# Input weights of two layers multiplied as high and low rounded parts, in a smaller ring of weight slots

## What is computed

```python
for layer in range(2):
    h = rms_norm(x, norm1_g[layer])
    sb, rw, mc, hc = h @ w_l[:, 0:768], h @ w_l[:, 768:1792], h @ w_l[:, 1792:2560], h @ w_l[:, 2560:3584]
    merged = None
    for n, y_n in enumerate((y_sb, y_rwkv, y_moba, y_hgrn)):       # the four mixers' outputs
        gate = jax.nn.sigmoid(h @ w_l[:, 3584 + 1024 * n:4608 + 1024 * n])
        term = gate * (y_n @ w_branch[layer, n])
        merged = term if merged is None else merged + term
    x = x + merged @ w_out[layer]
    h2 = rms_norm(x, norm2_g[layer])
    x = x + (silu(h2 @ w_ffn_gate[layer]) * (h2 @ w_ffn_up[layer])) @ w_ffn_down[layer]
```

## Time and profile before

| | us |
|---|---|
| median of 3 runs | 2181.14 (2177.85 to 2185.31) |
| profiled execution, its own time | 2176.91 |
| span in its profile | 2175.1 |

### The profile page before, as it was taken

How to read it: one execution, slowest core, us unless ns; L and a number is a source line. 1 busy time by engine, 2 the same in 40 slices (tenths; PEclk the granted TensorE clock), 3 DMA queues, 4 the chain that set the end, 5 groups by cost and what they waited for, 6 DMA issues and landing times.

```text
span 2175.1 us, 26152 instructions
## 1 busy us (share of the span) xinstructions
PE 1915.3 (88%) x11290; PEld 1442.1 (66%) x11290; DVE 771.7 (35%) x1306; ACT 524.1 (24%) x784; POOL 0.2 (0%) x4
## 2 busy tenths in 40 slices
PE   7999999999998999998999999998999876565654
PEld 6799876799997898766799998546888421111111
DVE  3442332655533533234355665323544200000001
ACT  2201121244432011211344463423442210000000
POOL 0000000000000000000000000000000000000000
PEclk9999999999999999999999999999999897677778
DMA  6222342465532223453745442211127799999997
GB/s 249 97 97 87 127 155 97 155 193 186 183 117 97 97 97 116 155 194 136 240 155 174 158 129 64 97 39 39 40 78 306 304 409 409 409 409 409 409 409 291
DMA packets 170323, 414.13 MB, mean 190 GB/s; under 512 B 4832, under 2 KB 61408, under 8 KB 166752
## 3 DMA queue, kind: packets, MB, share of 16 engines
q1 hardware_dynamic: 169488, 408.69, 50.8%
q10 hardware_dynamic: 720, 3.78, 0.4%
HBM read 411.41 MB, written 1.05 MB: 190 GB/s over the span
## 4 chain that ended last, share of the span: by engine, by line
PE 60%; DMA 20%; DVE 12%; ACT 7%; issue 1%; SPq 0%; ACTq 0%; DVEq 0%
PE ps L219 44%; PE ps L767 7%; DMA ring<-in_w_e_down_dram 5%; ACT rarena L213 5%; DMA high<-in_w_e_up_dram 5%; DVE rarena L178 4%; PE ps L1157 3%; PE ps L1514 2%; DVE low L178 2%; DMA ring<-in_w_e_up_dram 2%; DMA high<-in_w_e_down_dram 2%; DMA high<-in_w_e_gate_dram 2%; DMA ring<-in_w_e_gate_dram 2%; DVE high L178 2%; ACT high L213 1%
## 5 line engine op out<-in xcount | busy, mean ns | idle before, releaser
L219 PE MATMUL ps<-high,ring 128*128 128x256 f32 (+1 forms) x2016 | 482.7, 391 | 7.5 <-DMA ring<-in_w_in_dram 5.6
L219 PE MATMUL ps<-rarena 128*128 128x256 f32 (+1 forms) x3648 | 460.0, 288 | 9.6 <-DVE rarena L178 7.4
L219 PEld LDWEIGHTS ps<-rarena 128*128 128x128 f32 x3648 | 448.3, 192 | 19.6 <-DVE rarena L178 10.4
L219 PEld LDWEIGHTS ps<-high,ring 128*128 128x128 f32 x2016 | 376.4, 192 | 81.4 <-issue 20.2
L213 ACT ACTIVATE high<-ps 128x512 f32<-128x512 f32 (+2 forms) x210 | 103.3, 492 | 719.0 <-PE ps L1514 286.8
L1514 PE MATMUL ps<-high,low 128*32 128x512 f32 x1040 | 168.2, 780 | 103.0 <-DMA high<-in_w_e_up_dram 36.4
L178 DVE TENSOR_TENSOR rarena<-ring,rarena 128x2048 fp32r<-128x2048 f32 x76 | 167.3, 2201 | 137.5 <-ACT rarena L213 135.8
L1514 PEld LDWEIGHTS ps<-high,low 128*32 128x32 f32 x1040 | 32.1, 129 | 224.0 <-issue 62.0
L213 ACT ACTIVATE rarena<-ring 128x2048 fp32r<-128x2048 f32 x76 | 140.0, 1841 | 157.0 <-DMA ring<-in_w_ffn_up_dram 92.7
L178 DVE TENSOR_TENSOR high<-high,ps 128x512 f32<-128x512 f32 x52 | 35.7, 687 | 324.8 <-PE ps L1514 267.0
L219 PE MATMUL ps<-low,ring 128*128 128x256 f32 (+1 forms) x544 | 128.0, 392 | 14.9 <-DVE low L192 5.5
(11 more groups left out here) (149 smaller groups left out, 1364.9 us busy)
## 6 DMA issues: line engine op xcount, KB each, us to landing
ring<-in_w_in_dram SPq DMA_DIRECT2D x34, 2048.0 KB, 7.9
high<-in_w_e_gate_dram SPq DMA_DIRECT2D x22, 2048.0 KB, 24.0
high<-in_w_e_up_dram SPq DMA_DIRECT2D x22, 2048.0 KB, 24.1
high<-in_w_e_down_dram SPq DMA_DIRECT2D x21, 2048.0 KB, 24.0
ring<-in_w_mod_dram SPq DMA_DIRECT2D x12, 2048.0 KB, 8.7
ring<-in_w_ffn_gate_dram SPq DMA_DIRECT2D x22, 1024.0 KB, 5.4
ring<-in_w_ffn_up_dram SPq DMA_DIRECT2D x22, 1024.0 KB, 8.0
ring<-in_w_e_down_dram SPq DMA_DIRECT2D x11, 2048.0 KB, 24.3
```

Source lines behind the costliest of these rows:

```text
L219: ins = self.e.matmul(out, l, r, start=first and i == 0, stop=end and i == n - 1)
```

## The change

The 52 units of each layer are multiplied in parts, as the feed-forward part is. One piece is a block of 128 columns (128x1024 elements). ScalarE rounds it into slot 2 of the ring, which becomes the store of high parts (four places for blocks 0 to 27, two places after that, since half of the slot is needed), and VectorE writes the low part over the weights in their own slot. ScalarE does this for block u+2 in the first half step of unit u, VectorE in the second; from block 30 on it is block u+1. The input `h` is split as well, tile by tile during `rp`. In the mixers' stretch weights thus come through two slots, 0 and 1. The other half of slot 2 holds the branch weights `b1`, and then the modulation, in 24 loads of 1 MB one after the other, with a step of 4 matmuls each, spread over five gates after every 4 half steps (layer 0) or every 2 (layer 1). The branch weights `b0` go to slot 2 after the last mixer step. One `yield` of the RWKV mixer on ScalarE moves ahead of its `kn` work, and `MX_PLAN` is lengthened.

```diff
-            def units(l, nm, c0, w, parts):
-                wt = halves(wslot(f"{l}w{c0}")[:, 0:8 * w], 8)
-                PE.wait_ge(f"{l}w{c0}")
+            def units(l, nm, parts):
+                b_ = first_block[nm]
...
-                        prs = [(wt[:, j, o:o + 128], B.h[:, j, :]) for j in range(8)]
+                        ld, z, lo, hi_ = block_of(l, b_)
+                        PE.wait_ge(f"{l}lo{b_}")
+                        prs = [(hi_[:, j, :], lo[:, j, :], hh_[:, j, :], hl_[:, j, :]) for j in range(8)]
...
-                    PE.group(out, prs[0:4], end=False)
+                    PE.group3(out, prs[0:4], end=False)
...
+def blocks_ahead(u):
+
+    if u + 2 < TWO_PLACES + 2:
+        return [u + 2]
+    return [u + 1] if TWO_PLACES < u < BLOCKS - 1 else []
...
+            def block_high(l, b):
+
+                ld, z, low_, high_ = block_of(l, b)
+                A.wait_ge(ld, f"{fname(l - 1, FJOBS[-1])}.used" if l else None)
+                if b > 3:
+                    A.wait_ge(f"{l}blk{b - (4 if b < TWO_PLACES + 2 else 2)}.used")
+                A.act(fr(high_), z, Copy).then_inc(*A(f"{l}hi{b}"))
...
+            def block_low(l, b):
+
+                ld, z, low_, high_ = block_of(l, b)
+                V.wait_ge(f"{l}hi{b}")
+                low_part(low_, z, high_, f"{l}lo{b}")
...
-                for _ in mods:
-                    pass
+                ring_of[0] = NSLOT
+                held[2] = f"{l}fill.used"
                 for n in (0, 2, 3):
                     branch(l, n)
...
+                yield
                 A.wait_ge(f"{l}kn.ps")
                 A.wait_ge(f"{l}kmax")
                 A.act(R.t2, R.t2, Ln).then_inc(*A())
                 A.act(R.t1, R.t2, Exp, scale=-0.5).then_inc(*A(f"{l}kn"))
-                yield
...
+                h_low(7)
+                block_low(l, 0)
+                block_low(l, 1)
...
-MX_PLAN = 10 * [2] + [1], 14 * [2] + [1]
+BLOCKS, TWO_PLACES = 52, 28
+MX_PLAN = 13 * [2] + [1], 22 * [2] + [1]
```

More of the change, by code:

```diff
@@ L268, in mix, with woven, beside @@
             n += 1
-def woven(parts, other, counts):
-    for part, n in zip(parts, counts):
-        yield from part
-        for _ in range(n):
-            next(other, None)
-            yield
+def woven(parts, other, every):
+    n = 0
+    for part in parts:
+        for _ in part:
+            yield
+            n += 1
+            if n % every == 0:
+                next(other, None)
+                yield
[3 more added lines that the diff above has]
+    return [u + 1] if TWO_PLACES < u < BLOCKS - 1 else []
+def beside(steps, split, u, half):
+    for n, _ in enumerate(steps):
+        if n % 2 == half:
+            for b in blocks_ahead(u + n // 2):
+                split(b)
+        yield
 class Space:
@@ L391, in build @@
         B.xg = B.mg
+        place["top"] = GATES_AT
+        hh_ = shaped(rgates[:, :].bitcast(F32), [8, 256])
         B.gates = alloc(8, 256)
@@ L395, in build @@
         B.rs = alloc(256)
+        hl_ = shaped(rarena[:, place["top"] - LOW:place["top"] - LOW + 2048].bitcast(F32), [8, 256])
         B.h = alloc(8, 256)
@@ L443, in build @@
         free_to(mark)
-        gx = [B.gates] + [alloc(8, 256) for _ in range(2)]
+        gx = [at(23304, 8, 256)] + [alloc(8, 256) for _ in range(2)]
         H = Space()
@@ L679, in sync_program @@
                     table["par"] = (s_par, 32)
-                mods = modulation(l)
-                fill = [proj(l)] + [gate(l, n, ch) for n in (1, 0) for ch in range(2)]
-                fill += [woven([gate(l, n, ch) for n in (2, 3) for ch in range(2)], mods, MOD_COUNTS[l])]
-                mix([none(RW_STEPS)], fill, RW_PLAN, False)
-                branch(l, 1)
-                mix([none(HG_STEPS), none(SB_STEPS), none(MO_STEPS)], fill, MX_PLAN[l])
-                for _ in mods:
-                    pass
+                for nm, c0, w, parts in IN1:
+                    columns(f"{l}w{c0}", a["w_in"][l], c0, w)
+                for n, ch in GATES[0:3]:
+                    gate(l, n, ch)
+                held[HALF] = f"{l}blk{TWO_PLACES - 1}.used"
+                branch(l, 1, at=HALF)
+                mods = modulation(l)
+                gate(l, *GATES[3])
+                for i in range(4, 9):
+                    if i < 8:
+                        gate(l, *GATES[i])
+                    for _ in range(8 // MOD_EVERY[l]):
+                        next(mods, None)
+                ring_of[0] = NSLOT
+                held[2] = f"{l}fill.used"
                 for n in (0, 2, 3):
@@ L719, in sync_program @@
                 columns(f"to{half}", a["w_out_2"][0], 512 * half, 512)
[L721 removed]
+            ring_ = list(recent)
             order = ring_[:1] + [5, 6, 7, 8] + [3, 4] + ring_[1:]
@@ L790, in units @@
+                        PE.wait_ge(f"{l}lo{b_ + 1}")
+                        done = [b_, b_ + 1] if t else []
+                        tok = slice(128 * t, 128 * t + 128)
+                        prs = [(hh_[:, j, tok], hl_[:, j, tok], hi_[:, j], lo[:, j, :]) for j in range(8)]
+                        b_ += 2 * t
+                    PE.group3(out, prs[0:4], end=False)
                     yield
-                    PE.group(out, prs[4:8], first=False).then_inc(*PE(f"{l}{nm}{i}.ps"))
+                    PE.group3(out, prs[4:8], first=False).then_inc(*PE(f"{l}{nm}{i}.ps"))
@@ L792, in units @@
+                    for n in done:
+                        PE.mark(f"{l}blk{n}.used")
                     yield
-                PE.mark(f"{l}w{c0}.used")
+                PE.mark(f"{l}w{BLOCK[first_block[nm]][0]}.used")
             def proj(l):
                 for nm, c0, w, parts in IN1:
-                    yield from units(l, nm, c0, w, parts)
+                    yield from units(l, nm, parts)
             def gate(l, n, ch):
-                yield from units(l, f"g{n}{ch}", gate_col(n, ch), 512, "cccc")
+                yield from units(l, f"g{n}{ch}", "cccc")
@@ L1173, in tensor_program @@
                 mix([hgrn(l), stick(l), moba(l)], fill, MX_PLAN[l])
+                PE.mark(f"{l}fill.used")
                 branch(l, 0)
-                for _ in mods:
-                    pass
                 branch(l, 2, hgrn_turned)
```

134 lines of the change are left out of this document (80 added, 54 removed).

## The result

The changed kernel takes 2260.97 us (median of 4 runs, 2257.38 to 2261.64) where the kernel before takes 2180.83 beside it: the ratio is 1.036, with a 95% interval of 1.0341 to 1.0379. It is slower by 80 us. The prediction had 8 us slower and a range that ended at 2220. The direction was right, the size was not.

A forecast was written before the change was run, and what follows sets the result against it. TensorE's own work was taken as the bound, VectorE close behind after KBt. Costs of 68.7 us less 60.3 saved gave +8.4: 2185.3 us for an execution like the profiled one, 2189.5 beside the median; range 2158 to 2220.

The forecast's parts named there:

- theory A: Experiments' theory: rounding queued on VectorE and ScalarE ahead of short steps makes TensorE wait, each wait bringing a low clock.
- theory B: Experiments' theory: the loss comes from two slots and half a slot, whose loads land late.
- (a): Before kn: VectorE's low part of h and two blocks' low parts come first, delaying it 3.0 us a layer.
- (b): Before bo: ScalarE passes seven fill steps first, so TensorE waits, 6.5 us a layer with the low clock.
- (c), (d): VectorE after KBt, with six low parts, 4.2 and 1.8 us; one more low part before first X, 1.3 a layer.
- (e): Fourth level's D: late load g10, then a low part ahead of VectorE's X, cost 5.2 us a layer.
- (g): Other mixers: low parts queued ahead lengthen existing waits, and layer 0's pairs shift; 6.4 and 3.8 us.
- (h): Modulation through half a slot: waits for its chained loads, 0 us in layer 0 and 12.9 in layer 1.
- (i): Branch 0: its weights wait for slot 2, held until the last mixer step; 2.8 us a layer.
- first rival: Matmuls in parts run nearer their floor in short groups between float32 work, below 0.117 us each: 2159.5 us; chance 0.15.
- fourth: Rival: matmuls in parts get no cheaper at all, and the waits come: 2250 us; chance 0.02.
- third: Rival: the half slot's loads land late, 6.9 us for 1 MB and 10.3 for 2 MB: 2222 us; chance 0.30.

The follow-up runs named there:

- e7: Changed kernel's plan with float32 matmuls and no rounding, modulation joined to the half steps, ScalarE's kn step back ahead of the fill: 2202.0 us.
- e1: Changed kernel's slots, loads and order, but float32 matmuls straight from the slot and no rounding of weights or h: 2239.6 us.
- e2: Changed kernel with only each layer's first four blocks rounded, on ScalarE, and all 52 multiplied from those, for high and low parts alike: 2194.3 us.
- e3: Changed kernel without VectorE's low parts of the weights; ScalarE's high parts stay and are multiplied in their place: 2202.8 us.
- e14: Changed kernel without VectorE's low parts of the weights, modulation joined to the half steps, branch 0's weights in the half slot: 2172.6 us.
- e9: Changed kernel with the modulation joined to the half steps and branch 0's weights in the half slot: 2229.3 us.
- e5: Changed kernel with each modulation step joined to the half step behind it, not in a place of its own: 2246.1 us.
- e4: Changed kernel with the columns' loads an eighth and the modulation's a quarter as large, rounding and matmuls unchanged in number and shape: 2215.9 us.
- e8: Changed kernel with branch 0's weights loaded into the half slot after the last modulation step, instead of slot 2: 2244.2 us.
- e13: Changed kernel with float32 matmuls of constants put ahead of twelve of TensorE's waits: 2249.1 us.
- e10: Changed kernel with the low parts of the weights made by GpSimd instead of VectorE: 2258.3 us.

## Why the prediction was wrong

The runs make a ladder from one kernel to the other, in medians: the loads of the half slot and of branch 0, +21 (before to e7); the order, +38 (e7 to e1); the cheaper matmuls, -45 (e1 to e2); ScalarE's high parts, +8 (e2 to e3); VectorE's low parts, +58 (e3 to the changed kernel). Together +80. So theory A has 66 us, theory B 21, and the order, which neither named, 38. Each rung holds with those below it in place. Two were tried in another place too and came out alike: VectorE's low parts cost 57 us between e14 and e9, and the two placements 30 us there, for 32 with the low parts in. How the 38 us of the order split between `kn` and the modulation was not measured without the rounding; with it, the modulation's place is 15 us (e5). The prediction's own steps, idle time only, both layers, beside the trace of the changed kernel less that of before:

| step | predicted | measured |
|---|---|---|
| saving | -60.3 | -59.2 |
| (a) kn | 6.0 | 7.5 (6.74 and 8.53 for 3.55 and 4.25) |
| (b) bo | 9.4 | 9.3 (4.63 and 4.64) |
| (c), (d) to the first X | 8.6 | 21.0 (5.8 before `KBt`, 8.75 and 7.83 for 0.68 each) |
| (e) g10 | 6.8 | 11.1 (6.25 and 4.89) |
| (f) to the last fill | 2.0 | 2.3 (1.51 and 1.24 for 1.58, twice) |
| (g) the other mixers | 10.2 | 26 (what is left of 101.4) |
| (h) modulation | 11.0 | 19.5 (25.1 for 5.6) |
| (i) branch 0 | 5.6 | 4.5 (5.00 for 2.7, twice) |
| low clock | 8.8 | 43.0 |

By size, what failed is the low clock (34 us too little), (g) (16), (c) and (d) (12), (h) (8.5) and (e) (4). (Step (h)'s own terms, 4 + 18 - 9.4, give 12.6 and not the 12.9 of the sum, which changes nothing.)

**Right: the saving, (a), (b), (f) and (i) in size.** The matmuls in parts run at 0.118 us here, 0.120 in the earlier trace rows; the first rival began to win below 0.117 and did not come. Step (b) had the size and the cause, ScalarE's place behind the fill; e7 shows it from the other side, where the wait is gone.

**Step (c), (d): the place of one low part.** The prediction added one low part before the first X and took its 1.3 us. VectorE's timeline of the changed kernel shows what happened; under it stands TensorE's first X, before and in the changed kernel:

```profile
114.85 1.23 DVE L178 TENSOR_TENSOR rring<-ring,rring 128x1024 fp32r<-128x1024 f32 x1
116.18 1.49 DVE L178 TENSOR_TENSOR high<-ps,low 128x512 f32<-128x512 f32 x2
...
121.48 1.23 DVE L178 TENSOR_TENSOR high<-high,cst 128x1024 f32<-128x1024 f32 x1
122.74 0.86 DVE L184 TENSOR_SCALAR high<-high,low 128x256 f32<-128x256 f32 x2
123.71 1.22 DVE L178 TENSOR_TENSOR rring<-ring,rring 128x1024 fp32r<-128x1024 f32 x1
```

```profile
115.77 1.16 PE L767 MATMUL ps<-high 128*128 128x128 f32 x8 [0.68 <-DVE high L178]
...
127.78 1.48 PE L811 MATMUL ps<-high 128*128 128x128 f32 x6
```

TensorE's program has a half step (block 13, `sv`) ahead of the first X. Its low part stands behind the whole of VectorE's preparation of D, so TensorE could not start the half step while VectorE worked; it started it when all was done, at 125.08, and reached X only at 127.78. What X itself needs was done at 122.71 (in the kernel before the same operation ended at 115.71), so the place of the low part delays X by 5 us: 2.4 until the low part is done, and 2.7 for the half step, at the low clock. The rest of the wait of 8.75 us is what (c) had: VectorE works without a break from 96.19 to 124.93. The fill no longer fills: what was to be done during the wait now waits itself. The prediction counted the low part's duration and not that a covering half step turned into one that depends on the engine it was to cover. It also put nothing before `KBt`, where TensorE now waits 2.89 us in each layer: the low part at 88.94 us, which waited for ScalarE's high part, stands ahead of VectorE's work for it, and in e3 this wait is gone.

**Step (e) had the mechanism** (VectorE's answer to X queued behind a low part that waits for ScalarE and the load) and 3.4 us for 6.25 and 4.89; ScalarE could begin 9.1 us after the load's issue, not 8.0. e3 and e4 each take it away, so it needs both.

**Step (g) missed a change in the order.** It priced low parts ahead of waits that were there, and in layer 0 a shift of pairs. It did not price that a modulation step is now a place of its own, which holds 0.95 us of work (half of the earlier trace rows) where a mixer step expects 1.4 or 1.7 to hide VectorE's answer. That alone makes the waits of 3.89 and 1.9 us at the end, which stand in e1 too, without any rounding; e5 brings them to 0.80 and 0.50, and takes 12.8 us of idle time out of the two stretches in all. The rest of the row's 26 us was not taken apart.

**Step (h) was right in its longest waits** (behind a gate's load, 10.4 us from its issue, all three times) and took 4.2 us for what came to 6.70, 6.56 and 4.26, because TensorE was there earlier: 3.7, 3.9 and 6.2 us behind the gate's issue, where the step had 6.2 each time. In layer 0 it had no wait; there were 3.2 us. The estimate that the prediction quotes in step (e) from the Trainium skill (DMA: Bandwidth & Descriptors, section Anatomy of one DMA) is fitted there to DMAs that GpSimd issues, and these are SyncE's: 2 MB took 7.9 us and 1 MB 5.0 in the changed kernel, both longer than it gives.

**Step (i) hid a choice.** 2.8 us was the difference to before; the whole wait of 5 us and its clock could be avoided (e8, 17 us for both layers).

**The low clock is the largest single miss: 8.8 us predicted, 43.0 measured.** It was taken as 1.8 us for each wait of 2.7 us or more, from the two waits of the earlier trace rows, given to seven waits and taken back for two that went. In the traces it is a fairly even rate: over the runs of the table the low clock is 0.30 to 0.51 us for each us of idle time (0.30 before, 0.39 after, 0.51 in e13, where idle time was filled). In the mixers of layer 0 the clock fell to 0.50 behind single waits of 2.62, 3.56, 3.89 and 5.00 us and also behind pairs three us apart, 0.48 and 2.22, or 1.73 and 2.08, and stayed at 1.00 behind 1.41, 1.94 and 1.94 alone. The kernel before waited up to 2.52 us in the same mixers and kept its clock. But neither the length nor the closeness of waits decides by itself. In e9 the clock stayed at 1.00 behind a wait of 2.67 us (at 314.26) and fell behind one of 2.33 (at 349.70), and in layer 1 of the kernel before it fell to 0.50 behind this one:

```profile
967.32 1.19 PE L767 MATMUL ps<-high 64*128 64x128 f32 x8 [1.94 <-DVE high L178]
```

So a fixed price above a fixed length, which the prediction used, is refuted; the rate is an average over many waits, and what decides in a single case is open.

No rival had the reason. The fourth (matmuls in parts no cheaper, and the waits come, 2250 us) was nearest in time by chance: they did get cheaper, and the waits cost twice what it had. The third (loads that land late, 2222 us) is wrong too: the modulation's loads land after 5.0 us and the columns' after 7.9, by the page of the changed kernel, against 5.4 and 7.9 in the earlier trace rows. That the range ended at 2220 comes first from the low clock and from (g), then from (c) and (d).

## What to carry to other kernels

Work that is put in to cover a wait must not depend on the engine whose wait it covers, nor stand behind that engine's own queue: 58 of the 80 us are VectorE's low parts, although VectorE is busy 40% of the time. Price all the new standing still with its low clock, here some 0.4 us for each us on average, and not only the waits above some length. Before all of a kernel is changed, change the stretch where the cover is shown: a fifth of the blocks, in the levels, brought 12.6 us, where all of them cost 80.

## What was not expected of the hardware

**VectorE and GpSimd hold each other up.** While GpSimd makes low parts (2.40 us each), VectorE's operations with two SBUF operands take 946 for 425 ns, and three small ones of 128x2, 0.58 us together in the changed kernel, take 2.76 us at 106.12 in e10; those with an operand in PSUM are unchanged at 687. The Trainium skill (SBUF — State Buffer, section SBUF: two separate sides) has the two share a pair of ports under an "exclusive lock", held for a whole instruction, which VectorE's operations with two SBUF inputs take too while GpSimd reads SBUF. For those with two SBUF inputs the trace agrees: one that meets a GpSimd operation takes up to 2.45 us for 0.48. Its GPSIMD Engine Reference (section Engine selection) calls GpSimd some two times slower for operations of two inputs: 2.40 against 1.23 us here.

**Useless work made a kernel faster.** e13 adds over 130 matmuls of constants, 0.43 us each, and is 12 us faster, because the clock stayed at 2.4 GHz behind nine of the ten waits between `kn` and branch 1: the loss from it there fell from 20.3 to 1.6 us.
